# Second attention: probabilities and values as rounded parts and remainders, and two Fourier tiles moved into its last pair

## What is computed

```python
s_loc = jnp.einsum('bnqhd,binchd->bhnqic', qr, kb) * scale + bias   # 8 rows x 32 columns of keys
s_loc = jnp.where(mask, s_loc, NEG_INF)
s_ctx = jnp.einsum('bnqhd,bkhd->bhnqk', qr, k_ctx) * scale
p = jax.nn.softmax(jnp.concatenate([s_loc, s_ctx], axis=-1), axis=-1)
o = einsum(p_loc, vb) + einsum(p_ctx, v_ctx)
y_c = (o * silu(c_z)) @ w_br_c
y_f = (fourier_mix(f_u) * silu(f_z)) @ w_br_f
```

## Time and profile before

| | us |
|---|---|
| median of three executions | 2469.54 |
| the profiled execution | 2466.74 |
| its span in the trace | 2465.0 |
| first scores of the second attention to its last values | 1325.0 to 1664.0 |
| period of a pair with a next pair to prepare | 95.6 |
| last pair, from its first scores on | 45 |

### The profile page before, as it was taken

How to read it: one execution, slowest core, us unless ns; L and a number is a source line. 1 busy time by engine, 2 the same in 40 slices (tenths; PEclk the granted TensorE clock), 3 DMA queues, 4 the chain that set the end, 5 groups by cost and what they waited for, 6 DMA issues and landing times.

```text
span 2465.0 us, 30785 instructions
## 1 busy us (share of the span) xinstructions
PE 2343.0 (95%) x11310; PEld 1924.1 (78%) x11310; DVE 1113.7 (45%) x1381; ACT 775.2 (31%) x1095; POOL 863.9 (35%) x851
## 2 busy tenths in 40 slices
PE   4997888999999999999999999999999999999997
PEld 3776777777888888888778888887778888888886
DVE  7978887479631344124463343352211122222324
ACT  3237776032310222024424454452112111212210
POOL 1445554334433333223223323332223334333331
PEclk9998999999999999999999999999999999999999
DMA  7310001524111111111131111112011111111132
GB/s 305 116 50 28 17 26 49 217 94 179 51 51 43 51 51 43 51 60 49 39 111 61 55 36 54 36 30 91 22 40 44 49 51 52 51 47 41 49 128 77
DMA packets 48318, 166.02 MB, mean 67 GB/s; under 512 B 4480, under 2 KB 6272, under 8 KB 48128
## 3 DMA queue, kind: packets, MB, share of 16 engines
q1 hardware_dynamic: 48256, 165.19, 19.3%
HBM read 156.79 MB, written 8.39 MB: 67 GB/s over the span
## 4 chain that ended last, share of the span: by engine, by line
PE 80%; DVE 9%; issue 4%; ACT 3%; POOL 2%; DMA 1%; SPq 0%; DVEq 0%; ACTq 0%; POOLq 0%
PE acc L746 62%; PE turn L971 6%; PE bank L1035 3%; DVE ADA L1655 1%; DMA WF<-in_w 1%; PE bank L1013 1%; PE acc L959 1%; PE bank L848 1%; DVE HL L1635 1%; DVE acc L1812 1%; PE turn L640 1%; ACT EX L1258 1%; PE acc L724 1%; PE bank L1110 1%; PE bank L1107 1%
## 5 line engine op out<-in xcount | busy, mean ns | idle before, releaser
L746 PE MATMUL acc<-HH,WH 128*128 128x512 f32 x1600 | 497.4, 392 | 7.3 <-POOL WL L540 6.3
L746 PE MATMUL acc<-HL,WH 128*128 128x512 f32 x1600 | 493.9, 390 | 0.0
L746 PE MATMUL acc<-HH,WL 128*128 128x512 f32 x1600 | 493.8, 390 | 0.0
L537 POOL TENSOR_TENSOR WH<-WF,CON 128x16 fp32r<-128x16 f32 x186 | 52.7, 284 | 1206.1 <-PE acc L746 1024.5
L540 POOL TENSOR_TENSOR WL<-WF,WH 128x1024 fp32r<-128x1024 f32 (+2 forms) x186 | 439.5, 2363 | 15.5
L746 PEld LDWEIGHTS acc<-HH,WH 128*128 128x128 f32 x1600 | 300.5, 188 | 74.0 <-issue 6.9
L746 PEld LDWEIGHTS acc<-HL,WH 128*128 128x128 f32 x1600 | 301.3, 188 | 62.8
L746 PEld LDWEIGHTS acc<-HH,WL 128*128 128x128 f32 x1600 | 301.1, 188 | 62.8
L538 POOL TENSOR_SCALAR WH<-WF 128x1008 fp32r<-128x1008 f32 (+2 forms) x186 | 195.4, 1050 | 0.0
L1942 DVE SCALAR_TENSOR_TENSOR CV<-EV,VEC,CV 128x1023 f32<-128x1023 f32 x44 | 99.1, 2253 | 203.9 <-ACT CV L1334 203.1
L1870 DVE SCALAR_TENSOR_TENSOR XT<-acc,MOD,XT 128x1024 f32 (+1 forms) x34 | 43.6, 1284 | 233.1 <-PE acc L746 233.1
(11 more groups left out here) (373 smaller groups left out, 4100.2 us busy)
## 6 DMA issues: line engine op xcount, KB each, us to landing
WF<-in_w SPq DMA_DIRECT2D x150, 512.0 KB, 3.4
ADA<-in_ada SPq DMA_DIRECT2D x15, 1024.0 KB, 13.1
BIAS<-in_bias SPq DMA_DIRECT2D x16, 576.0 KB, 3.8
XT<-in_xT SPq DMA_DIRECT2D x16, 512.0 KB, 10.2
ADA<-in_ada SPq DMA_DIRECT2D x4, 2048.0 KB, 11.6
ADA<-in_ada SPq DMA_DIRECT2D x3, 2560.0 KB, 9.3
WF<-in_w SPq DMA_DIRECT2D x24, 256.0 KB, 2.6
ADA<-in_ada SPq DMA_DIRECT2D x8, 512.0 KB, 3.4
```

The source lines that it names most:

```text
L537: pool.tensor_tensor(h[:, 0:FEW], f[:, 0:FEW], zero.to_broadcast([P, FEW]), ALU.add).then_inc(w_hi, 1)
L746: last = pe.matmul(acc[:, slot, HALF * c:HALF * c + HALF], w[slot][:, k, :], x[:, k, HALF * c:HALF * c + HALF], start=(k == 0 and w is WH ...
```

## The change

Four parts.

1. The turned probabilities are kept as a rounded part (PT2H, by ScalarE as before) and a remainder (PT2L of 512 columns, PT2M of 128, by VectorE, `low_first` and `low_last`). The values by key are kept in the same way, both parts side by side in 128 columns of weights (VTOK2, `values_low`). `values2` becomes ten float32r matmuls of 128 weight columns x 128 moving columns. Its 128 output rows hold two halves, which VectorE adds (`tensor_copy`, `tensor_tensor`) before the gate's product. TensorE waits for `vtok2_low` and `pt2_low` where it waited for `vtok2_ready` and `pt2_ready`.
2. There are two buffers EX2 in place of four, and ScalarE now makes `turned_last(u)` before `exponents2(u + 2)`. `turn_last` always goes to bank 7 and stands at the end of the unit.
3. Keys and values are stored so that 4 rows of one column lie together. The values need one copy by ScalarE in place of four. The bias is kept in one buffer, loaded in three parts.
4. The first two tiles of the Fourier stage (N_F, N_F + 1) are computed in `turn` in the last pair, one chunk a unit (two in units 1 and 9, none in unit 8). Its loop has three rounds: `gemm`, `channels(it)`, `gemm`, `tokens(it)`, with `channels(3)` and `tokens(3)` behind it. The remainder CBL is made after the first `fold`.

```diff
+        VTOK2 = at("VTOK2", 9.5, [P, 2, NCH, P], F32R)
+        PT2H = [at(f"PT2H{s}", kb, [P, NKEY], F32R) for s, kb in enumerate((27.5, 117))]
+        PT2L = [at(f"PT2L{s}", kb, [P, HALF], F32R) for s, kb in enumerate((30, 135))]
+        PT2M = [at(f"PT2M{s}", kb, [P, P], F32R) for s, kb in enumerate((119.5, 137))]
+        EX2 = [at(f"EX2{s}", kb, [P, NKEY]) for s, kb in enumerate((112, 114.5))]
 # TensorE
+            def first_of_f(u):
+                if u in range(1, 8):
+                    if u == 1:
+                        pe.wait_ge(vtok2_low, 16)
+                    piece(N_F, 0, (0, 1) if u == 1 else (u,))
+                elif u in range(9, 16):
+                    if u == 9:
+                        pe.wait_ge(acc_read, N_F + 1)
+                    piece(N_F + 1, 1, (0, 1) if u == 9 else (u - 8,))
             def values2(it, u, last):
-                pe.wait_ge(pt2_ready, it * 32 + (2 * u + 2))
+                if u in (0, 8) or u == 12 and not last:
+                    pe.wait_ge(vtok2_low, it * 4 + {0: 3, 8: 4, 12: 5}[u])
+                pe.wait_ge(pt2_low, it * 32 + (2 * u + 2))
                 for k in range(NKEY // P):
                     kc = 4 * c + half + k if k < 3 else 4 * NB + k - 3
-                    mm = pe.matmul(bank7[0:HD, P:2 * P], VTOK2[:, j, kc, :], PT2[u % 2][:, P * k:P * k + P],
-                                   start=(k == 0), stop=(k == NKEY // P - 1))
+                    low = PT2L[u % 2][:, P * k:P * k + P] if k < 4 else PT2M[u % 2][:, :]
+                    for x in (PT2H[u % 2][:, P * k:P * k + P], low):
+                        mm = pe.matmul(bank7[:, P:2 * P], VTOK2[:, j, kc, :], x,
+                                       start=(k == 0 and x is not low), stop=(k == NKEY // P - 1 and x is low))
             turn_values(0, 0)
             turn_context(0).then_inc(pt2_done, 1)
+            pe.wait_ge(vtok2_low, 2)
             scores2(0, 0)
-            gemm(N_F, 0, HH, HL)
-            gemm(N_F + 1, 1, HH, HL)
-            channels(0)
-            with pe.Fori(1, 4) as it:
+            with pe.Fori(0, 3) as it:
 # ScalarE
             def attend2(it, last):
                 for u in range(16):
                     turned_first(it, u)
-                    if last and u > 0:
-                        turned_last(it, u, turn)
+                    turned_last(it, u)
+                    if u == 0:
+                        context_by_key(it, 1)
+                    elif u == 12 and not last:
+                        context_by_key(it + 1, 0)
                     if u < 14 or not last:
                         exponents2(it, u + 2)
-                    if not last or u == 0:
-                        turned_last(it, u, bank7)
                     if u == 0:
                         values_by_key(it, 1)
 # VectorE
+            def low_first(it, u):
+                dve.wait_ge(pt2_ready, it * 32 + (2 * u + 1))
+                dve.tensor_tensor(PT2L[u % 2][:, :], bank6[:, :], PT2H[u % 2][:, 0:HALF].bitcast(F32), ALU.subtract
+                                  ).then_inc(pt2_low, 1)
+            def values_low(p, j):
+                dve.wait_ge(vtok2_ready, p * 4 + (2 * j + 1))
+                dve.tensor_tensor(VTOK2[:, j, NCH - 2:, HD:P], ...
+                dve.wait_ge(vtok2_ready, p * 4 + (2 * j + 2))
+                dve.tensor_tensor(VTOK2[:, j, 0:NCH - 2, HD:P], turn[:, :].rearrange("p (c d) -> p c d", d=HD),
+                                  VTOK2[:, j, 0:NCH - 2, 0:HD].bitcast(F32), ALU.subtract).then_inc(vtok2_low, 1)
             def gather2(it, u):
-                dve.tensor_tensor(grid, bank7[0:HD, P:2 * P].rearrange("p (r c) -> p r c", c=QW), grid, ALU.mult
-                                  ).then_inc(o2_ready, 1)
+                dve.tensor_copy(O2[:, :], bank7[HD:P, P:2 * P]).then_inc(o2_half, 1)
+                dve.wait_ge(o2_half, it * 16 + (u + 1))
+                dve.tensor_tensor(O2[:, :], O2[:, :], bank7[0:HD, P:2 * P], ALU.add).then_inc(o2_ready, 1)
+                dve.wait_ge(o2_ready, it * 16 + (u + 2))
+                dve.tensor_tensor(grid, O2[:, :].rearrange("p (r c) -> p r c", c=QW), grid, ALU.mult).then_inc(gated2, 1)
                         largest2(it, u + 2)
+                    low_first(it, u)
                     if u > 0:
                         gather2(it, u - 1)
+                    low_last(it, u)
                     if u == 0:
+                        values_low(it, 1)
                         keys_low(it, 1, 1)
+                    if u == 12 and not last:
+                        values_low(it + 1, 0)
```

212 lines of the change are left out of this document (109 added, 103 removed).

## The result

| | before | after |
|---|---|---|
| time, median (range) | 2468.12 (2466.6 to 2470.85) | 2509.32 (2507.4 to 2513.47) |
| ratio, 95% interval | | 1.0167 [1.0151, 1.0183] |
| profiled execution, span | 2466.7, 2465.0 | 2507.4, 2505.6 |

Slower by 41 us, 1.7%, clear of the noise; 14.4 had been forecast, and the time lies outside the range. Times are in us throughout.

A forecast was written before the change was run, and what follows sets the result against it. TensorE, busy 95% of the span, was taken as the bound. Terms -10.2 + 2.4 + 7.0 + 3.5 + 4.7 + 7.0 = +14.4 on the median 2469.5 gave 2484 us; own range 2475 to 2492, overall range 2461 to 2502.

The forecast's parts named there:

- The pace of 0.112: In `values2`, each of the ten float32r matmuls was to take 0.112 us, 1.12 in all.
- rivals 1 and 2: `values2` matmuls cheap at 0.062, total 2467 or 2463 (chance 0.24); or at float32's 0.22, total 2528 (chance 0.11).
- rival 4: Last pair: chain shorter than summed, units 3.7 us, +9 in all, 2478; shares the forecast's chance of 0.50.
- No seams: Around `values2`: the float32 to float32r changes, some 0.34 us a unit, were to go.
- an ordinary unit: First three pairs: a unit with two chunks takes 5.0 us, gaining 0.31 in 33 units, -10.2 us.
- units 12 and 13: First three pairs: 14.6 us over these units instead of 13.0, +4.7 us in all.
- The rest of the Fourier stage has the same instructions in another order: Fourier stage beyond the moved tiles and costed loads: no change in time, costed at nothing.
- rival 3: TensorE's clock falls at each pair's start, half speed costing some 2.5 a time: +10, 2494; chance 0.15.
- the sum of the pair's start: From a pair's last fifth transpose to unit 1's in the next: 15.2 us instead of 11.7, +7.0 for two pairs.
- The last pair: From its start through Fourier tile N_F + 1: 76.5 us instead of 69.6, +7.0 us.
- The loop that was forecast right: Per-unit chain through four engines, closed by VectorE's addition before the fifth transpose: 4.2 us, setting last-pair units.
- the DFT load: Fourier stage: costed at nothing, with one tile of 10.9 us to hide in; 1 to 4 us if uncovered.

The follow-up runs named there:

- e7_once: Changed kernel with the Fourier channel products' wait on `acc_read` placed once ahead of the loop instead of in every round; 2503.96 us.
- e9_tail: e7_once with the Fourier stage's last projection tile moved between `tokens(2)` and `channels(3)`; 2502.55 us.
- e5_gather: Changed kernel with one swap in VectorE's order: gathering of the unit before goes ahead of `low_first`, the remainder of the first four turned tiles; 2492.53 us.
- e12_early: e10_best with the last pair's first pieces in unit 2; in other pairs VectorE gathers first, ScalarE evacuates (units 3, 7) ahead of the exponential; 2477.13 us.
- e6_psum: e5_gather with the sum of the two halves written back to its PSUM bank, so the gating product reads one operand from PSUM; 2496.18 us.
- e3_warm: Changed kernel with unused filler matmuls in gaps of units 0, 1 and 13 (13 not in the last pair) and around the first scores; 2513.36 us.
- e13_hybrid: First three pairs as e12_early; last pair with plain float32 probabilities and values, no pieces; Fourier stage as before the change; 2470.07 us.
- e14_early: e12_early with the last pair's first pieces back in unit 1; 2472.26 us.
- e10_best: Changed kernel with e5_gather, e9_tail, second head's query and last-key work out of pair starts, earlier first scores, values rounded earlier in unit 12; 2472.71 us.
- e2_unmoved: Changed kernel without part 4: no pieces in the last pair, Fourier loop and its two tiles as before; 2534.27 us.
- e4_seams: Kernel before with five float32 `values2` products replaced by ten float32r ones, remainders left out, result not the attention's; 2462.72 us.

## Why the prediction was wrong, point by point

The forecast's sum of 14.4 has three parts: +7.4 up to the last pair, +7.0 in it, 0 in the Fourier stage. Measured were +19.7 (with 0.3 of the first column), +11.0 and +9.9: 12.3, 4.0 and 9.9 more.

**Right.** The pace of 0.112 (0.111 to 0.112 from start to start), so rivals 1 and 2 fell, and so did rival 4, since the last pair's units didn't run at 3.7. The Trainium skill states about 0.081 for a stream of 128 columns ("TensorE: Matmul & The Clock Gate", section "Back-to-back issue gap"); it doesn't show here. No seams; 5.00 for an ordinary unit; 4.25 for a last-pair unit (4.2), with VectorE's addition as what ends the wait; unit 15 at 4.98 (4.75); 14.93 from a pair's last fifth transpose to that of unit 1 in the next (15.2); 14.1 over units 12 and 13 (14.6).

**"The rest of the Fourier stage has the same instructions in another order", costed at nothing: 9.9.** This step failed most plainly. The diff showed a new wait on `acc_read` in `channels` and no product between the third tile's token products and the fourth's channel products. The order was counted by its instructions, and nobody asked what each of them covers. e7_once and e9_tail show the parts: 3.8 of the wait of 7.30 was the added condition, needed for the first tile alone (3.4 by the stage); the missing cover was 4.9; 1.7 stayed.

**Up to the last pair: 12.3 more than forecast,** nearly all of it in the three pairs (up to the first fifth transpose it was 2.9, where some 2.7 had been forecast). Of it 4.7 are two falls of the clock (rival 3, with the right mechanism, priced at +10 for all starts). Units 4, 6 and 8 were forecast at 5.0, 5.0 and 5.1 and took 5.46, 5.70 and 5.62: 5.0 in three pairs (e5_gather mends 6, e12_early 4 and 8). And the sum of the pair's start ended at unit 1: unit 2 took 9.15, 1.4 more than 7.75. The operation that made it and unit 6 long, the gating product, stands in none of the forecast's sums: they end at the addition and put the product behind it at nothing. Its row, L2031 with 0.28 in the earlier trace rows, would not have warned either, since there one input is in PSUM; the changed one reads two operands from SBUF. The Trainium skill ("SBUF — State Buffer", section "SBUF: two separate sides") says that VectorE and GpSimd share a pair of ports, which a VectorE operation with two SBUF inputs and a GpSimd operation that reads SBUF take whole, one after the other. The runs agree: 14 products of 2.15 to 2.26 beside GpSimd's subtraction, none over 0.29 in e6_psum.

**The last pair: 11.0 for 7.0.** The ordinary units were right, to 0.05 (nine of 4.2 are 37.8, where the sum has 37.4). The two transposes at its start came after 16.4 and not 15.2: ScalarE's second table load (1.28) stood behind unit 0's fifth transpose, where in pair 2 it lay ahead of it, and the copy of the values began 9.4 after the last fifth transpose in place of 7.9. Unit 2 took 6.45 and not 4.9, with waits of 1.09 behind a gating product of 2.26 and of 1.24 for the addition. The clock was at 0.52 from 1649 to 1652, but e3_warm took as long without that fall.

**The loop that was forecast right was not unavoidable.** The prediction took VectorE's order as given. One swap of two calls took 16.8 out of the 41 (part of it the gating products that no longer meet the subtraction). The chain had the remainder of 0.68 ahead of an addition for which TensorE waited, while nobody waited for the remainder yet.

**The range.** Its upper end, 2502, held rival 3 (2494) and 0.12 for the matmul's price (+3). It had no room for a stage costed at nothing, though the text gave the DFT load there "1 to 4".

Open: what decides whether the clock falls behind a gap. The same gap did and did not, and in the pairs filler products made no difference that could be told. Open too is what makes the last pair's start longer in e13_hybrid and e14_early, and why the first column differs by up to 7 between kernels that are the same there.

## What to carry to other kernels

A product that gets cheaper by splitting its operands pays in remainders, and these lie on VectorE; look first for stretches where TensorE has other work under which they can lie (in the three pairs, where it had, e10_best gains 5.3 on the kernel before), and order VectorE's steps by who waits for them. Here the order of steps, with the products the same, decided between +41 and +3 us. When work is moved, go through the place that it left: what did it cover there, and does a new condition ahead of it hold for every iteration or for the first alone. And when an operand moves from PSUM to SBUF, a duration taken from the old row no longer covers what happens beside another engine; look in the old trace for an operation with the same places, and at its longest instance, not its mean.

## What the runs showed of the hardware that was not expected

- A VectorE product of 64x128 with both operands in SBUF takes 0.285 alone and 2.15 to 2.26 if it starts just behind the start of GpSimd's 2.37 subtraction; started ahead of it, 0.28 to 0.39 in 13 places of e5_gather. The query remainder (1.22 alone, SBUF as well) took 2.56 twice in e5_gather, where it had moved beside that subtraction, and in e14_early a remainder of the keys, 1.22 alone, took 3.37: it started 0.10 behind the subtraction of 2.38 and ended 1.1 after it.
- A gap of TensorE of 5.13 was followed by 9 us at a granted 0.50 to 0.52 (the 1.2 GHz level), in the last 6 of which TensorE was busy throughout; behind a gap of 2.51 in the same place the low level lasted some 3 us. Moving work out of that gap cost 4.6 in the whole. In e2_unmoved the last pair's units from 3 on, with 0.70 idle in 5.12, ran at that level; those of the kernel after, with 0.36 to 0.40 idle in 4.25, at the full one.
- Ten matmuls of 128 weight and 128 moving columns in float32r run 0.112 apart, as float32's records do, and the change between float32 and float32r products costs 0.3 a unit: e4_seams took it away and ordinary units fell from 5.33 to 5.03 (those of the last pair by 0.14, from 2.58 to 2.44).
